# Two output tiles of a feature-wise unit, computed in turn instead of one after the other

## What is computed

```python
h = rms_norm(x, norm_g[layer])
proj = h @ w_in[layer]
...
x = x + jnp.concatenate([o_diff, o_nsa], axis=-1) @ w_out[layer]
...
h = rms_norm_2(x, g_mix[layer])
proj = h @ w_in[layer]
...
merged = gates[..., :D_MODEL] * y_a + gates[..., D_MODEL:] * y_b
x = x + merged @ w_out[layer]
h2 = rms_norm_2(x, g_ffn[layer])
x = x + (jax.nn.silu(h2 @ w_ffn_gate[layer]) * (h2 @ w_ffn_up[layer])) @ w_ffn_down[layer]
return rms_norm_2(x, g_final)
```

## Time and profile before

| | |
|---|---|
| time, median of 3 runs | 1196.96 us (1196.86 to 1198.53) |
| profiled execution: span from first to last instruction | 1194.5 us |
| what lies around the span, against the median of the runs | 2.5 us |
| PE busy | 1142.2 us, 96% |
| PE matmuls at L1397 | 2712, of 5380 |
| POOL, ACT, DVE busy | 42%, 39%, 39% |
| mean granted TensorE clock | 0.986 |

### The profile page before, as it was taken

The page is one execution under the profiler, slowest core; times in us unless marked ns, Lnnn a source line. Parts: engine busy times, 40 slices in busy tenths (PEclk is TensorE's granted clock), DMA queues, the critical chain, the costliest instruction groups (busy, mean ns, idle before and its releaser), DMA issues.

```text
span 1194.5 us, 13900 instructions
## 1 busy us (share of the span) xinstructions
PE 1142.2 (96%) x5380; PEld 910.6 (76%) x5380; DVE 470.4 (39%) x971; ACT 470.3 (39%) x776; POOL 496.7 (42%) x222
## 2 busy tenths in 40 slices
PE   5999999898999989999999899998999999999996
PEld 4777778676776877788888678887888888878785
DVE  3574410387743231893520593713000000024544
ACT  6322332577765352522332673325212221223333
POOL 4331344654543523144434583442344434434441
PEclk9999999989999999999999899999999999999998
DMA  6324422000000623132332102232332332232321
GB/s 218 106 71 141 122 83 94 1 1 1 1 2 1 211 63 106 36 102 76 105 106 97 45 2 71 71 106 71 106 97 79 105 105 85 90 105 74 120 71 71
DMA packets 82480, 96.14 MB, mean 80 GB/s; under 512 B 8056, under 2 KB 66640, under 8 KB 82424
## 3 DMA queue, kind: packets, MB, share of 16 engines
q1 hardware_dynamic: 81864, 93.27, 24.6%
q0 software_dynamic: 560, 2.12, 0.5%
HBM read 93.26 MB, written 2.12 MB: 80 GB/s over the span
## 4 chain that ended last, share of the span: by engine, by line
PE 88%; DMA 3%; DVE 2%; ACT 2%; issue 2%; POOL 1%; SPq 1%; DVEq 0%; ACTq 0%; POOLq 0%
PE bank L1397 47%; PE bank L1454 21%; PE bank L1541 5%; PE bank L1500 5%; PE bank L1521 3%; DMA raw<-in_w_in 3%; PE bank L1650 1%; PE bank L1414 1%; PE bank L1478 1%; PE bank L1613 1%; POOL w_lo L627 1%; SPq L572 1%; PE bank L1576 1%; PE bank L1539 1%; PE bank L1533 1%
## 5 line engine op out<-in xcount | busy, mean ns | idle before, releaser
L627 POOL TENSOR_TENSOR w_lo<-raw,w_hi 128x2048 fp32r<-128x2048 f32 (+3 forms) x59 | 263.8, 4472 | 423.8 <-ACT w_hi L721 423.8
L1397 PE MATMUL bank<-h_hi,w_hi 128*128 128x512 f32 (+2 forms) x904 | 354.4, 392 | 1.5 <-POOL w_lo L627 1.4
L1397 PE MATMUL bank<-h_hi,w_lo 128*128 128x512 f32 (+2 forms) x904 | 352.0, 389 | 0.0
L1397 PE MATMUL bank<-h_lo,w_hi 128*128 128x512 f32 (+2 forms) x904 | 352.0, 389 | 0.0
L1397 PEld LDWEIGHTS bank<-h_hi,w_hi 128*128 128x128 f32 (+2 forms) x904 | 169.3, 187 | 39.0 <-POOL w_lo L627 1.8
L1397 PEld LDWEIGHTS bank<-h_lo,w_hi 128*128 128x128 f32 (+2 forms) x904 | 169.3, 187 | 36.3 <-issue 1.0
L1397 PEld LDWEIGHTS bank<-h_hi,w_lo 128*128 128x128 f32 (+2 forms) x904 | 169.3, 187 | 35.8
L721 ACT ACTIVATE w_hi<-raw 128x2048 fp32r<-128x2048 f32 (+3 forms) x59 | 109.8, 1861 | 208.4 <-PE bank L1454 138.5
L701 POOL TENSOR_TENSOR w_lo<-raw,w_hi 128x2048 fp32r<-128x2048 f32 x22 | 101.3, 4606 | 147.7 <-ACT w_hi L980 74.2
L1454 PE MATMUL bank<-w_hi,h_hi 128*128 128x512 f32 x368 | 144.6, 393 | 4.9 <-DVE h_lo L1269 2.5
L1454 PE MATMUL bank<-w_hi,h_lo 128*128 128x512 f32 x368 | 143.8, 391 | 0.0
(11 more groups left out here) (175 smaller groups left out, 1155.2 us busy)
## 6 DMA issues: line engine op xcount, KB each, us to landing
raw<-in_w_in SPq DMA_DIRECT2D x31, 1024.0 KB, 5.3
raw<-in_w_ffn_gate SPq DMA_DIRECT2D x11, 1024.0 KB, 5.3
raw<-in_w_ffn_up SPq DMA_DIRECT2D x11, 1024.0 KB, 5.3
raw<-in_w_out SPq DMA_DIRECT2D x8, 1024.0 KB, 5.1
raw<-in_w_ffn_down SPq DMA_DIRECT2D x8, 1024.0 KB, 5.0
raw<-in_cmp_w SPq DMA_DIRECT2D x4, 1024.0 KB, 5.7
raw<-in_w_ffn_down SPq DMA_DIRECT2D x4, 768.0 KB, 4.4
xres<-in_x SPq DMA_DIRECT2D x4, 512.0 KB, 4.9
```

Source lines behind the costliest of these rows:

```text
L627: nc.gpsimd.tensor_tensor(w_lo[:, s % 2, 0:size], raw[:, u.n % 2, 0:size], w_hi[:, s % 2, 0:size].bitcast(F32), ALU.subtract).then_inc(lo_ ...
L1397: ins = mm(dst, w_pair[w], h_pair[h], start=start and p == 0, stop=stop and p == 2)
```

## The change

The two tiles of a pair share one loop over k and the three products, and the matmuls alternate between their banks. The increments of `tile_done` come at the last two matmuls of the pair. `free_bank` is called for both tiles ahead of the first matmul. `between()` comes after half of the pair's k tiles, which in a unit of two tiles is after 24 matmuls, as before. In the feed-forward loop both gate tiles, and both up tiles, are computed likewise, and the wait is for both banks at once. The count of matmuls, their shapes and all other engines' instructions are the same.

```diff
                 if u.tiles:
-                    for j, (c0, m, kind, idx) in enumerate(u.tiles):
-                        t = u.tile + j
-                        free_bank(t)
-                        for k in range(u.nk):
-                            if j == 0 and fresh[0] is not None:
+                    for pair in (u.tiles[0:2], u.tiles[2:4]):
+                        j0 = u.tiles.index(pair[0]) if pair else 0
+                        for j in range(len(pair)):
+                            free_bank(u.tile + j0 + j)
+                        for k in range(u.nk if pair else 0):
+                            if j0 == 0 and fresh[0] is not None:
                                 pe.wait_ge(h_lo_done, fresh[0] + u.k0 + k + 1)
                             h = u.k0 + k
-                            ins = three(bank[t % 4][0:m, :], (hi[:, k, c0:c0 + m], lo[:, k, c0:c0 + m]),
-                                        (h_hi[:, h, :], h_lo[:, h, :]), k == 0, k == u.nk - 1)
-                        ins.then_inc(tile_done, 1)
-                        if j == 0:
-                            between()
+                            for p, (x, w) in enumerate(((h_hi, hi), (h_lo, hi), (h_hi, lo))):
+                                for j, (c0, m, kind, idx) in enumerate(pair):
+                                    ins = mm(bank[(u.tile + j0 + j) % 4][0:m, :], w[:, k, c0:c0 + m], x[:, h, :],
+                                             start=k == 0 and p == 0, stop=k == u.nk - 1 and p == 2)
+                                    if k == u.nk - 1 and p == 2:
+                                        ins.then_inc(tile_done, 1)
+                            if j0 == 0 and k == u.nk // 2 - 1:
+                                between()
...
                             for m in range(2):
                                 if first:
                                     free_bank(t0 + 2 * j + m)
-                                else:
-                                    pe.wait_ge((gsilu, act_done)[j], f * 2 + (m - 1))
-                                for k in range(ND):
...
-                                ins.then_inc(tile_done, 1)
+                            if not first:
+                                pe.wait_ge((gsilu, act_done)[j], f * 2)
+                            for k in range(ND):
...
+                                for p, (x, w) in enumerate(((h_hi, hi), (h_lo, hi), (h_hi, lo))):
+                                    for m in range(2):
+                                        ins = mm(bank[(t0 + 2 * j + m) % 4][:, :], w[:, k, P * m:P * m + P], x[:, k, :],
+                                                 start=k == 0 and p == 0, stop=k == ND - 1 and p == 2)
+                                        if k == ND - 1 and p == 2:
+                                            ins.then_inc(tile_done, 1)
```

More of the change, by code:

```diff
@@ L1669, in ffn_step @@
                                     free_bank(t0 + 2 * j + m)
-                                else:
-                                    pe.wait_ge((gsilu, act_done)[j], f * 2 + (m - 1))
-                                for k in range(ND):
[L1673 to L1677, removed]
-                                ins.then_inc(tile_done, 1)
+                            if not first:
+                                pe.wait_ge((gsilu, act_done)[j], f * 2)
+                            for k in range(ND):
+                                if first and j == 0:
+                                    pe.wait_ge(h_lo_done, at["h"] - ND + k + 1)
+                                for p, (x, w) in enumerate(((h_hi, hi), (h_lo, hi), (h_hi, lo))):
[4 more added lines that the diff above has]
+                                            ins.then_inc(tile_done, 1)
                     ffn_step(0, first=True)
```

## The result

The changed kernel takes 1222.53 us (median of 4 runs, 1219.72 to 1223.41) against 1197.74 us before in the same session (4 runs, 1196.86 to 1200.04): a ratio of 1.0195 over the runs, with a 95% interval of 1.0175 to 1.0216 (the quotient of the two medians, 1.0207, lies inside). It is slower; whether by a little less or a little more than 2% stays open. The profiled execution has a span of 1217.9 us at a mean granted clock of 0.975, against 1194.5 at 0.986; 23.4 us have come in between.

The account below looks back on a forecast made before the run. PE, busy 96% of the span, was taken to bound the kernel. Alternation saves 0; terms 9.0 + 3.0 + 1.65 + 0.55 + 2.95 + 2.15 = 19.3 us raise the span from 1194.5 to 1213.8, median 1216.3; range 1206 to 1223.

Parts of the forecast that it names:

- Part 1: 2688 matmuls at L1397 alternating banks: 0 us saved, pace stays 0.2265 us; upper bound of gain 35.8 us.
- R1: Rival: the 13 ns per matmul are a same-bank cost that alternation removes, giving 1180 us; 6 in 100, partial gain 2.
- R2: Rival: small gaps in PE's stream make the clock fall more often, +27 us, 1243 us; 3 in 100.
- (a): `cmp_kv` and `diff_k` 0 wait for DVE to release both tiles' banks: two stalls of 4.5 us, +9.0 us.
- R3: Rival: stalls at `cmp_kv` and `diff_k` 0 are shorter and the clock stays up, 1207 us; 7 in 100.
- (b): Granted clock falls to half after the two 4.5 us stalls at `cmp_kv` and `diff_k` 0: +3.0 us, bounds 0 and 6.
- (c): Averages of `diff_k` 0, `diff_k` 1 and `nsa_q` 0 wait for ACT's square of the first tile: +1.65 us; `nsa_q` 1: 0.
- (d): ACT copies both `nsa_v` tiles before rounding weights for `diff_z`, one copy more in front of PE's wait: +0.55 us.
- (e): At `k_ik_v_iw`, DVE's first-tile copies delay the indexer's first matmul, +1.55 us; likely clock fall, +1.4 us (bounds 0 and 3).
- (f): Small waits: before the feed-forward network +0.6, `index_q` +0.4, loop end +0.65, second attention stage +0.5; sum +2.15 us.

## Why the prediction was right, and where its sizes were off

The direction, the mechanism and its places were right; 1216 was forecast and 1222.5 came, inside the range, near its upper end. Against the spans it is 19.3 us forecast and 23.4 measured. By the steps:

**Part 1 (0 us).** Confirmed: 0.22675 us after, 0.22676 before, and the kernel without turns takes the same time as the one with them. R1 is out. So is R2: the granted clock is 1.00 over the whole feed-forward loop in turn (844 to 1083 us), and the kernel with this loop alone in turn takes what before takes.

**(a) +9.0 us.** 9.1: twice 4.78 us pass between the starts around a wait, where 0.23 are due. The chain through DVE was shown by leaving one link out. R3 is out with it. `diff_k` 0 starts at 69.39 all the same, beyond the 66.5 to 68.0 of the forecast, and that is (b).

**(b) +3.0 us for two falls of the clock.** Mis-sized. The place was right, the price not: by the distances between the same matmuls of both traces, the first cost 2.6 us and the second 3.0, so 5.6. I had taken the price from a fall after 2.46 us of idle, where half clock lasted for seven matmuls; after 4.4 us of idle it lasted for thirteen and fourteen. The step that failed is to take the price from a single fall: behind the same wait of 4.39 us half clock lasted for only seven matmuls in the kernel with both waits and no turns. What decides this stays open.

**(c) +1.65 us.** About 0.8: +0.6, +0.3 and +0.4, and 0.5 less at `nsa_q` 1. **(d) +0.55.** About 0.2: the wait for POOL went from 0.74 to 0.95 us.

**(e) +1.55 and +1.4 us.** +1.4 for the later start; the fall of the clock came, and cost 3.0 (14 matmuls of the indexer, 0.43 instead of 0.22 us apart), again twice my price. In the kernel with both waits and no turns it didn't come.

**(f) +2.15 us.** +0.85 at `index_q`, +0.35 at the second attention stage, +0.65 and +0.5 around the feed-forward loop: 2.35.

What is left is the clock at places I didn't price. Two stretches at half clock, in the attention stage and ahead of the feed-forward network, lasted longer than before and added 1.1 and 1.1 us. The one after the loop didn't come, though PE had waited for 2.96 us there, which gave 1.5 back:

```profile
1086.90 0.47 PE L1458 MATMUL bank<-w_hi,h_hi 128*128 128x512 f32 x1 [2.96 <-DVE h_lo L1269]
...
1088.60 0.39 PE L1458 MATMUL bank<-w_hi,h_lo 128*128 128x512 f32 x1
```

Seven matmuls took 1.70 us here, and 3.12 in the earlier trace rows after a shorter wait. After the same wait it did fall in the kernel with the feed-forward loop alone in turn (1066.45, above), so that these 1.5 us are luck. The size of a clock term is known to a factor of two at best, and whether it comes at all isn't known either. All in all the clock gave 5.6 + 3.0 + 1.1 + 1.1 - 1.5 = 9.3 us, where 4.4 had been forecast: 4.9 too little. The waits were 13.9 us instead of 14.9, and 0.2 us are spread over other places. That the forecast of 1216 came within 0.6% rests on the waits, which were read from rows; the clock terms could have come out several microseconds either way.

## What to carry to other kernels

Before interleaving two accumulations, read the distance between starts where the old order changes bank anyway: if it is the same there as inside a tile, alternation has nothing to give. Computing two tiles together makes both complete at the end, so whatever read or released the first under the second's matmuls comes onto the path; look for the places where a bank's release takes nearly as long as its next use is away (here 0.5 us of slack at `cmp_kv`), and keep those tiles apart. A new wait of some microseconds on TensorE also costs the matmuls after it that run at half clock, so the stall's own length isn't the whole price. Give such a term a range from several falls (0 to 3 us each in these traces), not one number.

## What the runs showed of the hardware

- With rounded fp32 operands a matmul takes a fixed 13.3 ns beside its columns at full clock: 0.2267 us for 512 columns, 0.120 for 256. It doesn't depend on whether the neighbour writes the same bank, nor does it fall with 64 instead of 128 stationary columns (0.2300 us over the loop). At half clock it isn't seen.
- The Trainium skill (TensorE: Matmul & The Clock Gate, "Back-to-back issue gap") gives N / 2.4 + 2.5 ns for a single matmul by itself, and about 131 ns for each of a stream of weight loads and matmuls with N = 512. The runs here show 13.3 ns in the place of its 2.5, at both lengths, and nothing near 131 ns (226.7).
- After two waits of 4.4 us the granted clock was at 0.57 and 0.54 for the next seven microseconds. After one of 2.96 us it stayed at 1.00 (1088.60, above), and after one of 2.95 us in another kernel it fell three matmuls later (1066.45). Behind waits of 4.39 us half clock lasted for seven matmuls in one place and for thirteen or fourteen in the others.
